# Tokens and memory loaded already turned, beside the plain copies

## The chip, the cores and the metric

The program runs on one NeuronCore of a Trainium2 chip. The metric is the device time of one launch in microseconds (us); its median of 3 runs before the change is 2022.22 us (2019.41 to 2022.70).

## The reference, cut to what matters

256 tokens of 1024 numbers go through a transformer block (`first_block`) and two further layers whose last part picks 16 rows per head and token out of a table of experts. What the change touches is the beginning of the first block:

```
h     = rmsnorm(x, mix_norm_g)          # (256, 1024), g a gain per feature
proj  = h @ w_in                        # queries, keys, values of two attentions, memory queries, gates
mem_n = rmsnorm(mem, mem_norm_g)        # (256, 1024)
mkv   = mem_n @ w_mem_kv                # keys and values of the memory
```

`rmsnorm(x, g)` is x times the inverse root of the mean of its squares, times g. A product needs its left operand with features along the partitions, that is, turned. The kernel multiplies by g (one number a partition in the turned form) before the product and by the inverse root (one number a token) when a product is evicted.

## The kernel before, in words

Tokens are handled as two tiles of 128. A stage is a generator in a program for each engine: `block(0)` and `block(1)` ("B0", "B1") are the first block on one tile each, "G0" (`first_gates`) the gate products of tile 0, "M00" to "M11" the mixers of the later layers. A generator yields between steps. A planner (`make_plan`) runs all generators once on paper with prices for instructions (`Meter`: a transpose 0.16 us at L164, a VectorE operation 0.2 us and 0.00107 us a column, L171) and writes for TensorE, VectorE and ScalarE one fixed order of steps; the same run chooses for each of the 512 expert rows of a partition, which are gathered by GpSimd, when it is fetched, into which buffer (`gather`, L660), and whether TensorE or VectorE adds it up (`on_which`, L589). An engine waits for what a step needs, in that order.

All weights come as slabs of 128 x 2048 numbers (1 MB) through a ring of six, issued by SP in the order in which TensorE takes them; slab n waits until slab n - 6 is used. Small loads are written by hand into SP's program among them, and all of SP's loads land in the order of their issue.

Stage B0 on TensorE (L876): eight dummy products (`turns`, L788, with START[0]) on a blank tile; eight transposes of `x3[:, 0]` through PSUM (`turn_tile`, L796), which VectorE multiplies by the gain and writes to `hT` (L1589); nine more dummies; five column tiles of w_in (two slabs each, `token_tile`); sixteen transposes of memory (L902), which VectorE writes to `memT`; the memory products (L912); normalised heads turned, attention; eight transposes of the second half of x (`early_turns`, L1014, evicted into `x1T`, which shares its place with part of `memT`); then the attention output o is turned and goes through the branch products (L960). `early_products` (L1028) later use `x1T` to begin stage B1's first two column tiles in gaps.

ScalarE squares x for the inverse root (`rms_tile`), and every eviction of a column tile needs it. VectorE makes the rotary angles, sums squares of the heads and norms them; group 2 of these waits for the memory products. SP's first loads (L2361 to L2365) are the identity, x, the gains and other vectors (`vecs`), positions and constants; after the fourth slab come the head gains, masks and memory, after the sixth the second half of x (L2308 to L2313).

Of the kernel before, what the change touches and what calls it, by code (L numbers as in the profile page):

```python
# [14 lines left out]
P = 128  # L15
# [12 lines left out]

EARLY_BANKS = (5, 1)
START, NORM, MIX = (8, 9), (0, 2), (0, 0, 3, 2, 4)  # L30
ADD = ((0, 2), (6, 7), (0, 1), (6, 7))
# [30 lines left out]
class Signals:  # L62
# [24 lines left out]
    def at(self, name, *key):  # L87
        if self.by_name:
            return self.name(name, *key)
        return self.sem(name), self.values.get((name, key), 1)  # L90
# [138 lines left out]
def program(nc, T, out):  # L229
    ctx = ExitStack()  # L230
    with ctx:
# [489 lines left out]
        def tensor_program(pe, measured=False):  # L721
# [154 lines left out]
            def block(t):  # L876
# [9 lines left out]
                if t == 0:  # L886
                    w.wait_ge(sig.sem("blank"), 1)
                    turns(b_[5], START[0], diag[:, 0:128])
                    w.wait_ge(sig.sem("l_id"), 16)
                    yield from turn_tile(s, x3[:, t, :], b_[6:8], "turned_v", (sig.sem("l_x0"), 16), "h")  # L890
                    turns(b_[5], START[1])
                    w.wait_ge(*at("turned_v", s, "h", 1))
                else:
                    w.wait_ge(*at("x1T_over"))
                    w.wait_ge(*at("qkv", 1, 1))
# [4 lines left out]
                if t == 0:  # L900
                    for u in range(2):
                        yield from turn_tile(s, mem3[:, u, :], b_[6:8], "turned_v", (sig.sem("l_m"), 16), "m%d" % u)  # L902
                    w.wait_ge(*at("turned_v", s, "m1", 1))
                    for part in range(2):
                        weights, n = take(s)
                        wk = blocks_of(weights, 4, 512)
                        for u in range(2):
                            b = b_[2 + u]
                            if part == 0:
                                wait_bank(b)  # L910
                            for k in range(4):
                                ins = pe.matmul(bank(b), memT[:, 4 * part + k, 128 * u:128 * u + 128], wk[:, k, :],  # L912
                                                start=(part == 0 and k == 0), stop=(part == 1 and k == 3))
                            if part == 0 and u == 1:
                                ins.then_inc(*up("half", "mem_kv"))
                                consumed[n] = ("half", "mem_kv")
                            if part == 1:
                                ins.then_inc(*up("mem_kv", u))
                                bank_free[b] = at("mem_out", u, 1)
                            yield  # L920
                    consumed[n] = ("mem_kv", 1)

                def heads():
                    w.wait_ge(*at("normed", t))
                    for i, (blocks, _) in enumerate(query_key_groups(s, t)):
                        b = b_[i % 2]
                        wait_bank(b)
                        for j, c in enumerate(blocks):
                            ins = pe.transpose(bank(b)[:, 128 * j:128 * j + 128], raw[:, 128 * c:128 * c + 128], ident)
                        ins.then_inc(*up("qk_turn", t, i))  # L930
                        bank_free[b] = at("qk_out", t, i)
                        yield
                    if t == 0:
                        b = b_[0]
                        wait_bank(b)
                        for i, (j, u) in enumerate(((0, 0), (0, 1), (1, 0), (1, 1))):
                            ins = pe.transpose(bank(b)[:, 128 * i:128 * i + 128], mem_k[:, u, 128 * j:128 * j + 128], ident)
                        ins.then_inc(*up("qk_turn", t, 4))
                        bank_free[b] = at("qk_out", t, 4)
                    yield from attention(s, block_units(s, t), [at("qk_out", t, 4 if t == 0 else 3)])  # L940

                yield from heads()
                if t == 0:
                    early_turns()
                yield from turn_tile(s, scr_[:, 0:1024], b_[6:8], "turned_a", at("att_out", s, 2), "o")
# [67 lines left out]

            def early_turns():  # L1014

                w.wait_ge(sig.sem("l_x1"), 16)
                w.wait_ge(*at("gates_out", 0, 4))
                for h in range(2):
                    b = EARLY_BANKS[h]
                    wait_bank(b)  # L1020
                    for i in range(4):
                        ins = pe.transpose(bank(b)[:, 128 * i:128 * i + 128], x3[:, 1, 512 * h + 128 * i:512 * h + 128 * i + 128], ident)
                    ins.then_inc(*up("turn", "B1", "h", h))
                    bank_free[b] = at("turned_v", "B1", "h", h)

            early_weights = {}

            def early_products(s, c, first, last):  # L1028

                b = room["B1"].bank[c]  # L1030
                for k in range(first, last):
# [4 lines left out]
                    if k == 0:  # L1036
                        w.wait_ge(*at("turned_v", "B1", "h", 1))
                        wait_bank(b)
# [10 lines left out]
            def first_gates():  # L1049

                b_, hTt = room["B0"].bank, hT_tile("B0")
                w.wait_ge(*at("turned_v", "B0", "h", 1))
                for c in range(6):
                    after = at("gates_out", 0, c - 2) if c > 1 else at("mem_out", 1, 1) if c else at("turned_v", "B0", "h", 1)
                    yield from token_tile("G0", (b_[5], b_[3])[c % 2], hTt, "gates", 0, c, after=after)
# [159 lines left out]
        def scalar_program(act, measured=False):  # L1215
# [78 lines left out]
            def block(t):  # L1294
# [6 lines left out]
                else:  # L1301
# [3 lines left out]
                    yield  # L1305
                    yield from rms_tile(s, row_y[0], "h", (sig.sem("l_x1"), 16), at("turned_v", "B0", "m1", 1))
                    begin(s)
# [104 lines left out]
            def mixer(l, t):  # L1412
# [42 lines left out]
                if l == 0:  # L1455
                    before.append(at("turned_v", "B0", "m1", 1))
                else:
                    before.append(at("dot", 128 * t + 127))
# [25 lines left out]
            def recurrence(l, t):  # L1484
# [4 lines left out]
                if l == 0:  # L1489
                    w.wait_ge(*at("turned_v", "B0", "m1", 1))  # L1490
                else:
                    w.wait_ge(*at("dot", 128 * t + 127))
# [66 lines left out]
        def vector_program(v, measured=False):  # L1559
# [29 lines left out]
            def turn_tile(s, key, gain, banks, dst):  # L1589

                for h in range(2):
# [5 lines left out]
                    yield  # L1597
                yield

            def attention(s, t, units, out):  # L1600
# [113 lines left out]
            def block(t):  # L1714
# [5 lines left out]
                if t == 0:  # L1720
                    begin(s)
                    yield from turn_tile(s, "h", vecs[:, V_MIX:V_MIX + 8], b_[6:8], hTt)
                yield from rms_tile(s, "h", "rms", s)
# [80 lines left out]
                if t == 0:  # L1804
                    for u in range(2):
                        yield from turn_tile(s, "m%d" % u, vecs[:, V_MEM:V_MEM + 8], b_[6:8], memT[:, :, 128 * u:128 * u + 128])

# [17 lines left out]
                if t == 0:  # L1825
                    yield from turn_tile("B1", "h", vecs[:, V_MIX:V_MIX + 8], EARLY_BANKS, x1T)
                for br in range(3):
# [438 lines left out]
        def load_program(sp):  # L2266
# [32 lines left out]
            def block(t):  # L2299
# [5 lines left out]
                for c in range(4 if t else 0, 10):  # L2305
                    slab(S_QKV + c)
                    if t == 0 and c == 3:
                        sp.dma_start(rows, T["rows"][:, 0:384]).then_inc(sig.sem("l_r"), 16)  # L2308
                        sp.dma_start(const[:, K_MC:K_ONE], T["const"][:, K_MC:K_ONE]).then_inc(sig.sem("l_k"), 16)
                        sp.dma_start(early[:, 0:1024], T["const"][:, K_END - 1024:K_END]).then_inc(sig.sem("l_k"), 16)  # L2310
                        sp.dma_start(mem3, T["mem"].rearrange("(t p) d -> p t d", p=P)).then_inc(sig.sem("l_m"), 16)
                    if t == 0 and c == 5:
                        sp.dma_start(x3[:, 1, :], x_in[:, 1, :]).then_inc(sig.sem("l_x1"), 16)  # L2313
                    yield
                if t == 0:
# [3 lines left out]
                    for br in range(3):  # L2319
                        yield from branch(br)  # L2320
                    small(0)
                else:
# [37 lines left out]

            sp.dma_start(const[:, 0:K_MC], T["const"][:, 0:K_MC]).then_inc(sig.sem("l_id"), 16)  # L2361
            sp.dma_start(x3[:, 0, :], x_in[:, 0, :]).then_inc(sig.sem("l_x0"), 16)
            sp.dma_start(vecs[:, :], T["vecs"]).then_inc(sig.sem("l_v"), 16)
            sp.dma_start(posi[:, :], T["pos"]).then_inc(sig.sem("l_p"), 16)
            sp.dma_start(const[:, K_ONE:], T["const"][:, K_ONE:K_END - 1024]).then_inc(sig.sem("l_c"), 16)  # L2365
            stage = {"B0": block(0), "G0": first_gates(), "B1": block(1)}
# [168 lines left out]
```

## Time and profile before

| what | value |
|---|---|
| median of 3 runs | 2022.22 us |
| the profiled execution's own time | 2018.75 us |
| its span, first to last instruction | 2016.9 us |
| TensorE matmul busy | 1770.3 us (88%) |
| VectorE busy | 1282.6 us (64%) |
| ScalarE busy | 870.7 us (43%) |
| bytes moved by DMA | 770.14 MB, mean 382 GB/s |

One execution was recorded. Busy times of engines overlap, and a share of the whole span is a mean over stages with different limits; the views by stretch tell which limit holds where. A product of 128 x 512 shows as two matmul records of the trace, a transpose as one.

### The profile page before, as it was taken

How to read it: one execution, taken by the hardware profiler on the slowest of the kernel's cores; microseconds unless marked ns; L12 is line 12 of the kernel's file. 1: busy time of each engine (PE TensorE's matmuls, PEld its weight loads, DVE VectorE, ACT ScalarE, POOL GpSimd, SP SyncE). 2: the span in 40 equal slices, each digit the busy share in tenths (PEclk: the TensorE clock that was granted, in tenths of full speed). 3: DMA queues.
4: the chain of work that ended last, by engine and by line, in shares of the span. 5: the costliest groups of instructions: out<-in, count | busy, mean ns of one | idle time of the engine just before them, and what ended most of it. 6: DMA issues, size and time to landing. Idle time of an engine off the chain costs nothing.

```text
span 2016.9 us, 21790 instructions
## 1 busy us (share of the span) xinstructions
PE 1770.3 (88%) x7152; PEld 1000.8 (50%) x7152; DVE 1282.6 (64%) x3502; ACT 870.7 (43%) x2188; POOL 584.8 (29%) x517
## 2 busy tenths in 40 slices
PE   9999999999899989888779979977898888777776
PEld 5459865764487446455225535622364474222222
DVE  4324337678565448786786857688677688865444
ACT  2423214344488433723344473344445625443333
POOL 0000000033232225334343324344433335443331
PEclk9999999999999989999899999999999989999999
DMA  9669877479999999999999999999999999999996
GB/s 391 217 256 362 299 278 250 161 286 419 419 419 419 420 420 418 419 418 395 419 420 420 419 419 409 419 419 420 420 420 419 379 419 420 420 419 420 420 420 267
DMA packets 108385, 770.14 MB, mean 382 GB/s; under 512 B 12144, under 2 KB 12656, under 8 KB 16368
## 3 DMA queue, kind: packets, MB, share of 16 engines
q0 software_dynamic: 73728, 536.90, 64.4%
q1 hardware_dynamic: 34544, 231.85, 29.7%
q8 instruction: 56, 0.92, 0.2%
q14 instruction: 57, 0.47, 0.1%
HBM read 767.65 MB, written 1.05 MB: 381 GB/s over the span
## 4 chain that ended last, share of the span: by engine, by line
DMA 48%; PE 38%; DVE 6%; ACT 4%; issue 2%; POOL 1%; SPq 0%; DVEq 0%; POOLq 0%; ACTq 0%
DMA arena<-in_peer_dram,eidx 17%; DMA ring<-in_peer_dram,eidx 13%; PE psum L1189 10%; PE psum L754 9%; DMA kv<-in_peer_dram,eidx 9%; PE psum L777 7%; DMA ring<-in_slabs_dram 5%; PE psum L989 5%; DMA early<-in_peer_dram,eidx 4%; PE psum L1006 2%; PE psum L960 1%; DVE ring L2108 1%; DVE arena L2108 1%; ACT diag L1534 1%; PE psum L852 1%
## 5 line engine op out<-in xcount | busy, mean ns | idle before, releaser
L2261 POOL DMA_INDIRECT arena<-in_peer_dram,eidx x205 | 238.0, 1161 | 789.7 <-DVE eidx L1980 409.9
L1189 PE MATMUL psum<-arena,diag 128*128 128x512 f32 x704 | 344.5, 615 | 69.2 <-ACT diag L1534 68.0
L1524 ACT ACTIVATE wexp<-wexp 128x1 f32<-128x1 f32 x512 | 103.2, 201 | 669.6 <-DVE wexp L2108 658.8
L2108 DVE CUSTOM_DVE_ANT_0 arena<-arena,osb 128x1024 f32<-128x1024 f32 x205 | 250.2, 1223 | 147.1 <-DMA arena<-in_peer_dram,eidx 143.7
L1189 PE MATMUL psum<-ring,diag 128*128 128x512 f32 x568 | 277.8, 614 | 55.3 <-ACT diag L1534 54.6
L2261 POOL DMA_INDIRECT ring<-in_peer_dram,eidx x152 | 170.5, 1122 | 281.5 <-PE psum L1189 241.6
L754 PE MATMUL psum<-ring,hT 128*128 128x512 f32 x528 | 241.2, 604 | 11.8 <-DMA ring<-in_slabs_dram 10.4
L1189 PEld LDWEIGHTS psum<-arena,diag 128*128 128x128 f32 x704 | 124.8, 192 | 252.0 <-ACT diag L1534 147.7
L2108 DVE CUSTOM_DVE_ANT_0 ring<-ring,osb 128x1024 f32<-128x1024 f32 x152 | 185.6, 1222 | 100.5 <-DMA ring<-in_peer_dram,eidx 98.8
L1189 PE MATMUL psum<-kv,diag 128*128 128x512 f32 x368 | 184.3, 626 | 41.7 <-ACT diag L1534 37.8
L1189 PEld LDWEIGHTS psum<-ring,diag 128*128 128x128 f32 x568 | 100.9, 192 | 204.0 <-ACT diag L1534 117.6
L1534 ACT ACTIVATE diag<-const,wexp 128x128 f32<-128x128 f32 x455 | 182.6, 401 | 16.3 <-PE psum L1189 1.5
L2261 POOL DMA_INDIRECT kv<-in_peer_dram,eidx x104 | 117.6, 1131 | 241.3 <-PE psum L1189 185.8
L2108 DVE CUSTOM_DVE_ANT_0 kv<-kv,osb 128x1024 f32<-128x1024 f32 x104 | 127.1, 1223 | 86.2 <-DMA kv<-in_peer_dram,eidx 85.5
L777 PEld LDWEIGHTS psum<-hT,ring 128*128 128x128 f32 x1344 | 159.5, 195 | 28.1 <-issue 17.1
L989 PEld LDWEIGHTS psum<-hT,ring 128*128 128x128 f32 x1408 | 162.6, 192 | 14.2 <-issue 8.6
L777 PE MATMUL psum<-hT,ring 128*128 128x128 f32 x1344 | 161.5, 278 | 8.2 <-DMA ring<-in_slabs_dram 6.6
L989 PE MATMUL psum<-hT,ring 128*128 128x130 f32 x1408 | 163.5, 276 | 3.7 <-DMA ring<-in_slabs_dram 1.9
L754 PEld LDWEIGHTS psum<-ring,hT 128*128 128x128 f32 x528 | 98.7, 192 | 133.8 <-issue 111.7
L1527 ACT ACTIVATE wexp<-wexp,sm 128x1 f32<-128x1 f32 x512 | 150.7, 294 | 16.6
L1189 PEld LDWEIGHTS psum<-kv,diag 128*128 128x128 f32 x368 | 66.1, 194 | 141.3 <-ACT diag L1534 80.8
L1524 ACT ACT_TABLE_LOAD x82 | 105.2, 1283 | 1.5
(340 smaller groups left out, 2023.6 us busy)
## 6 DMA issues: line engine op xcount, KB each, us to landing
ring<-in_slabs_dram SPq DMA_DIRECT2D x200, 1024.0 KB, 5.4
ring<-in_slabs_dram SPq DMA_DIRECT2D x8, 768.0 KB, 4.2
kept<-in_slabs_dram SPq DMA_DIRECT2D x4, 1024.0 KB, 13.7
arena<-in_peer_dram,eidx POOLq DMA_INDIRECT x205
ring<-in_peer_dram,eidx POOLq DMA_INDIRECT x152
ring<-in_slabs_dram SPq DMA_DIRECT2D x4, 512.0 KB
kk<-in_keys_dram SPq DMA_DIRECT2D x2, 1024.0 KB
kv<-in_peer_dram,eidx POOLq DMA_INDIRECT x104
```

The lines of the kernel that those rows point to most:

```text
L754: ins = pe.matmul(bank(b), hT_[:, k, :], wk[:, k % 4, :], start=(k == 0), stop=(k == 7))
L777: ins = pe.matmul(bank(b)[:, 128 * i:128 * i + 128], wk[:, k, 128 * (i % 2):128 * (i % 2) + 128], hT_[:, k, :], start=(k == 0), stop=(k == 7))
L852: ins = pe.matmul(bank(b)[:, c0:c0 + 64], p3[:, h, c, :], u.v(h, c), start=(c == 0), stop=(c == nb - 1))
L960: ins = pe.matmul(bank(b), oT[:, k0 + k, :], wk[:, k, :], start=(k == 0), stop=(k == kb - 1))
L989: ins = pe.matmul(bank(b)[:, 256 * gv:256 * gv + 130], wk[:, k, 128 * gv:128 * gv + 128], hTe[:, k, :], start=(k == 0), stop=(k == 7))
L1006: ins = pe.matmul(bank(b), act[:, f, :], wk[:, k, 512 * h:512 * h + 512], start=(f == 0), stop=(f == 21))
L1189: ins = pe.matmul(bank(b), diags_of(n), pair(slot_of[n])[:, 1024 + 512 * h:1536 + 512 * h], start=(k == 0), stop=(k == 127))
L1524: act.activation(wn, wn, ACT.Gelu_apprx_tanh).then_inc(*up("gelu", n))
L1527: act.activation(wn, wn, ACT.Copy, scale=gate[t][:, k:k + 1]).then_inc(*up("weight", n))
L1534: act.activation(diags_of(n), ident, ACT.Copy, scale=wn).then_inc(*up("diag", n))
L2108: v.tensor_tensor_reduce(out=row, in0=row, in1=row_y[t], scale=1.0, scalar=0.0, op0=ALU.mult, op1=ALU.add, accum_out=wexp[:, c:c + 1]).the ...
L2261: pool.indirect_dma_start(pair(i), None, tables, bass.IndirectOffsetOnAxis(ap=eidx[:, 128 * t + k:128 * t + k + 1], axis=0)).then_inc(sig. ...
```

## The change

Two arrays are added to the inputs: x and memory with features along the partitions. TensorE no longer turns inputs; `hT`, `memT` and `x1T` are loaded and then multiplied in place by the gain in one VectorE operation each (`scale_input`). The plain x and memory are still loaded, since the squares and the residual need them. The dummy products become fifteen in one run. Waits on the old evictions become waits on `scaled_in`, or on `mem_sq` where they guard the buffer of plain memory. Small loads change places, and the wait for the identity moves to the heads.

```
+START, NORM, MIX = 15, (0, 2), (0, 0, 3, 2, 4)

 tensor, block(0):
-                    turns(b_[5], START[0], diag[:, 0:128])
-                    w.wait_ge(sig.sem("l_id"), 16)
-                    yield from turn_tile(s, x3[:, t, :], b_[6:8], "turned_v", (sig.sem("l_x0"), 16), "h")
-                    turns(b_[5], START[1])
-                    w.wait_ge(*at("turned_v", s, "h", 1))
+                    turns(b_[5], START, diag[:, 0:128])
+                    w.wait_ge(*at("scaled_in", "x0"))
...
-                    for u in range(2):
-                        yield from turn_tile(s, mem3[:, u, :], b_[6:8], "turned_v", (sig.sem("l_m"), 16), "m%d" % u)
-                    w.wait_ge(*at("turned_v", s, "m1", 1))
+                    w.wait_ge(*at("scaled_in", "mem"))
...
-                if t == 0:
-                    early_turns()

 vector:
+            def scale_input(name, turned, gain, n):
+                w.wait_ge(sig.sem("l_v"), 16)
+                w.wait_ge(sig.sem("l_t" + name), 16)
+                g_ = gain.unsqueeze(2).to_broadcast([P, 8, n])
+                v.tensor_tensor(turned, turned, g_, ALU.mult).then_inc(*up("scaled_in", name))
...
-                    for u in range(2):
-                        yield from turn_tile(s, "m%d" % u, vecs[:, V_MEM:V_MEM + 8], b_[6:8], memT[:, :, 128 * u:128 * u + 128])
+                    scale_input("mem", memT, vecs[:, V_MEM:V_MEM + 8], 256)
+                    yield

 loads, first:
-            sp.dma_start(const[:, 0:K_MC], T["const"][:, 0:K_MC]).then_inc(sig.sem("l_id"), 16)
-            sp.dma_start(x3[:, 0, :], x_in[:, 0, :]).then_inc(sig.sem("l_x0"), 16)
+            sp.dma_start(hT[:, 0:1024], T["xT"][0]).then_inc(sig.sem("l_tx0"), 16)
             sp.dma_start(vecs[:, :], T["vecs"]).then_inc(sig.sem("l_v"), 16)
-            sp.dma_start(posi[:, :], T["pos"]).then_inc(sig.sem("l_p"), 16)
-            sp.dma_start(const[:, K_ONE:], T["const"][:, K_ONE:K_END - 1024]).then_inc(sig.sem("l_c"), 16)

 loads, behind slab c of w_in (0 to 9):
+   c == 1: x (first half), positions, constants
    c == 3: head gains            + identity, memory (masks gone from here)
+   c == 7: memT
-   c == 5: x (second half)
+   c == 9: masks, x (second half)

 loads, behind the last branch slab:
+                    w.wait_ge(*at("mem_kv", 1))
+                    sp.dma_start(arena[:, 7168:8192], T["xT"][1]).then_inc(sig.sem("l_tx1"), 16)
                     small(0)
```

`small(0)` is six loads for the later layers (L2278). Stage B1's scaling of `x1T` stands in VectorE's program where the evictions of `early_turns` stood.

## Rows read from the trace of the kernel before

**Rows 1.** The page: DMA rate in 40 slices; the chain by engine

```profile
GB/s 391 217 256 362 299 278 250 161 286 419 419 419 419 420 420 418 419 418 395 419 420 420 419 419 409 419 419 420 420 420 419 379 419 420 420 419 420 420 420 267
...
DMA 48%; PE 38%; DVE 6%; ACT 4%; issue 2%; POOL 1%; SPq 0%; DVEq 0%; POOLq 0%; ACTq 0%
```

**Rows 2.** Two stretches: length, busy time (instructions) by engine, clock, DMA share, rate

```profile
40.00:60.00 20.00, 20.00 (x60) 9.76 (x59) 10.54 (x25) 0.94 (x3) 0.00 (x0) 1.00 0.82 326
...
100.00:120.00 20.00, 19.21 (x91) 11.74 (x90) 5.17 (x19) 10.86 (x23) 0.00 (x0) 1.00 0.57 191
```

**Rows 3.** Timeline of the start: start, length, engine, line, operation, tiles, idle before

```profile
0.75 0.38 SPq L2361 DMA_DIRECT2D const<-in_const_dram  x1
...
1.00 3.78 PE L794 MATMUL psum<-diag 128*128 128x128 f32 x16 [1.00 <-POOL diag L2247]
1.19 0.42 SPq L2362 DMA_DIRECT2D x<-in_x_dram  x1
...
4.80 1.06 ACT L1223 ACTIVATE scr<-x 128x1024 f32<-128x1024 f32 x1 [2.78 <-DMA x<-in_x_dram]
...
6.65 2.28 PE L794 MATMUL psum<-const 128*128 128x128 f32 x18
...
9.12 13.97 PE L754 MATMUL psum<-ring,hT 128*128 128x512 f32 x32 [0.19 <-DMA ring<-in_slabs_dram]
...
13.31 0.26 ACT L1292 ACTIVATE junk<-junk 128x64 f32<-128x64 f32 x1 [1.54 <-DVE junk L1704]
...
24.11 16.15 PE L754 MATMUL psum<-ring,hT 128*128 128x512 f32 x37 [1.02 <-DMA ring<-in_slabs_dram]
```

**Rows 4.** DMA issues at 0.75, 1.65, 4.0 and 16.2: size, us to landing

```profile
const<-in_const_dram SPq DMA_DIRECT2D x1, 64.0 KB, 1.9
...
vecs<-in_vecs_dram SPq DMA_DIRECT2D x1, 193.0 KB, 3.7
...
ring<-in_slabs_dram SPq DMA_DIRECT2D x1, 1024.0 KB, 10.0
...
ring<-in_slabs_dram SPq DMA_DIRECT2D x1, 1024.0 KB, 17.3
```

**Rows 5.** Chain of waits, 44 to 135 us: start, length, engine and line

```profile
44.98 0.87 PE psum L805 x8
...
115.86 0.88 PE psum L1022 x8
116.73 0.87 PE psum L805 x8
...
132.36 1.72 PE psum L1039 x4
```

**Rows 6.** Timelines of VectorE and SP near 116 us; the issue at 116.3

```profile
115.96 0.42 DVE L1646 TENSOR_TENSOR scr<-psum,sm 128x256 f32<-128x256 f32 x1 [4.74 <-PE psum L852]
...
113.89 0.43 SPq L2282 DMA_DIRECT2D wf<-in_wf_dram  x1
...
115.81 0.98 SPq L2295 DMA_DIRECT2D kept<-in_slabs_dram  x2
...
kept<-in_slabs_dram SPq DMA_DIRECT2D x1, 1024.0 KB, 12.9
```

**Rows 7.** VectorE's groups by shape, 20 to 80 us: busy, mean ns

```profile
L1768 DVE TENSOR_TENSOR scr<-scr,early 128x384 f32<-128x384 f32 x4 | 2.2, 558 | 0.1
...
L1768 DVE TENSOR_TENSOR arena<-arena,early 128x256 f32<-128x256 f32 x2 | 0.9, 426 | 0.1
```

**Rows 8.** Later stretches, columns as in rows 2

```profile
430.00:440.00 10.00, 9.51 (x23) 4.03 (x22) 7.38 (x29) 5.95 (x12) 7.20 (x6) 1.00 1.01 419
...
900.00:930.00 30.00, 28.35 (x196) 23.62 (x197) 20.30 (x67) 6.86 (x21) 8.12 (x7) 1.00 0.95 377
...
1580.00:1610.00 30.00, 26.68 (x78) 12.88 (x78) 21.60 (x33) 15.10 (x39) 9.40 (x9) 0.94 0.93 351
...
2000.00:2017.00 17.00, 7.93 (x16) 2.71 (x16) 7.44 (x16) 5.71 (x15) 0.00 (x0) 0.91 0.10 38
```

More of the change, by code:

```diff
@@ L27 @@
 LAG = 3
-EARLY_BANKS = (5, 1)
-START, NORM, MIX = (8, 9), (0, 2), (0, 0, 3, 2, 4)
+START, NORM, MIX = 15, (0, 2), (0, 0, 3, 2, 4)
 ADD = ((0, 2), (6, 7), (0, 1), (6, 7))
@@ L924, in heads @@
                     w.wait_ge(*at("normed", t))
+                    w.wait_ge(sig.sem("l_id"), 16)
                     for i, (blocks, _) in enumerate(query_key_groups(s, t)):
@@ L1012, in block @@
                     bank_free[b_[6 + h]] = at("ffn_x", t, h)
[L1014 to L1024, printed above, removed]
             early_weights = {}
@@ L1036, in early_products @@
                     if k == 0:
-                        w.wait_ge(*at("turned_v", "B1", "h", 1))
+                        w.wait_ge(*at("scaled_in", "x1"))
                         wait_bank(b)
@@ L1051, in first_gates @@
                 b_, hTt = room["B0"].bank, hT_tile("B0")
-                w.wait_ge(*at("turned_v", "B0", "h", 1))
+                w.wait_ge(*at("scaled_in", "x0"))
                 for c in range(6):
-                    after = at("gates_out", 0, c - 2) if c > 1 else at("mem_out", 1, 1) if c else at("turned_v", "B0", "h", 1)
+                    after = at("gates_out", 0, c - 2) if c > 1 else at("mem_out", 1, 1) if c else at("scaled_in", "x0")
                     yield from token_tile("G0", (b_[5], b_[3])[c % 2], hTt, "gates", 0, c, after=after)
@@ L1305, in block @@
                     yield
-                    yield from rms_tile(s, row_y[0], "h", (sig.sem("l_x1"), 16), at("turned_v", "B0", "m1", 1))
+                    yield from rms_tile(s, row_y[0], "h", (sig.sem("l_x1"), 16), at("mem_sq", 1))
                     begin(s)
@@ L1455, in mixer @@
                 if l == 0:
-                    before.append(at("turned_v", "B0", "m1", 1))
+                    before.append(at("mem_sq", 1))
                 else:
@@ L1489, in recurrence @@
                 if l == 0:
-                    w.wait_ge(*at("turned_v", "B0", "m1", 1))
+                    w.wait_ge(*at("mem_sq", 1))
                 else:
@@ L1721, in block @@
                     begin(s)
-                    yield from turn_tile(s, "h", vecs[:, V_MIX:V_MIX + 8], b_[6:8], hTt)
+                    scale_input("x0", hTt, vecs[:, V_MIX:V_MIX + 8], 128)
+                    yield
                 yield from rms_tile(s, "h", "rms", s)
@@ L1804, in block @@
                 if t == 0:
-                    for u in range(2):
-                        yield from turn_tile(s, "m%d" % u, vecs[:, V_MEM:V_MEM + 8], b_[6:8], memT[:, :, 128 * u:128 * u + 128])
+                    scale_input("mem", memT, vecs[:, V_MEM:V_MEM + 8], 256)
+                    yield
                 yield from norms(1)
@@ L1825, in block @@
                 if t == 0:
-                    yield from turn_tile("B1", "h", vecs[:, V_MIX:V_MIX + 8], EARLY_BANKS, x1T)
+                    scale_input("x1", x1T, vecs[:, V_MIX:V_MIX + 8], 128)
+                    yield
                 for br in range(3):
@@ L2306, in block @@
                     slab(S_QKV + c)
+                    if t == 0 and c == 1:
+                        sp.dma_start(x3[:, 0, :], x_in[:, 0, :]).then_inc(sig.sem("l_x0"), 16)
+                        sp.dma_start(posi[:, :], T["pos"]).then_inc(sig.sem("l_p"), 16)
+                        sp.dma_start(const[:, K_ONE:], T["const"][:, K_ONE:K_END - 1024]).then_inc(sig.sem("l_c"), 16)
                     if t == 0 and c == 3:
                         sp.dma_start(rows, T["rows"][:, 0:384]).then_inc(sig.sem("l_r"), 16)
+                        sp.dma_start(const[:, 0:K_MC], T["const"][:, 0:K_MC]).then_inc(sig.sem("l_id"), 16)
+                        sp.dma_start(mem3, T["mem"].rearrange("(t p) d -> p t d", p=P)).then_inc(sig.sem("l_m"), 16)
+                    if t == 0 and c == 7:
+                        sp.dma_start(arena[:, 6144:8192], T["memT"]).then_inc(sig.sem("l_tmem"), 16)
+                    if t == 0 and c == 9:
                         sp.dma_start(const[:, K_MC:K_ONE], T["const"][:, K_MC:K_ONE]).then_inc(sig.sem("l_k"), 16)
                         sp.dma_start(early[:, 0:1024], T["const"][:, K_END - 1024:K_END]).then_inc(sig.sem("l_k"), 16)
-                        sp.dma_start(mem3, T["mem"].rearrange("(t p) d -> p t d", p=P)).then_inc(sig.sem("l_m"), 16)
-                    if t == 0 and c == 5:
                         sp.dma_start(x3[:, 1, :], x_in[:, 1, :]).then_inc(sig.sem("l_x1"), 16)
@@ L2518 @@
     arrays = {
-        "x": a["x"][0], "mem": a["mem"][0], "pos": a["positions"][0].reshape(2, P).T,
+        "x": a["x"][0], "xT": a["x"][0].reshape(2, P, 8, P).transpose(0, 3, 2, 1).reshape(2, P, 1024),
+        "mem": a["mem"][0], "memT": a["mem"][0].reshape(256, 8, P).transpose(2, 1, 0).reshape(P, 2048), "pos": a["positions"][0].reshape(2, P).T,
         "const": constants(), "vecs": vecs, "rows": np.broadcast_to(row, (P, row.size)),
```

## The prediction

> **What bounds the kernel now.** I read the page's slices first [rows 1]. DMA is below full until about a quarter of the span and then flat at 420 GB/s to the last slice; DMA has 48% of the chain that ended last and TensorE 38%. So there are two regimes, and the change lies wholly in the first. The table by stage [rows 2] shows what the first regime waits for: from 40 to 60 us TensorE is busy for all of 20.00 us and DMA for 0.82, from 100 to 120 us 19.21 us against 0.57. The chain of waits [rows 5] is then one TensorE group behind another, each starting where the last ended, and the only pause before 117 us that a load ends is the 1.02 us ahead of 24.11 us, until a slab of weights had landed [rows 3]. The late windows [rows 8] show the second regime: from 430 us DMA is at 1.01, with a dip at 900 to 930 us (377 GB/s), one at 1580 to 1610 us (351), a small one between, and 17 us at the end with hardly a transfer. There the end is the moment of saturation, plus a fixed number of bytes over the rate, plus dips, plus the tail. A microsecond won ahead of 430 us is won at the end, provided the dips stay as they are.
>
> **The start.** Time now goes, by [rows 3, 4], into a first come, first served queue: the first load, 64 KB, is issued at 0.75 us and takes 1.9; x of 512 KB is issued at 1.19 and ScalarE starts on it at 4.80; vecs is there at 1.65 + 3.7 = 5.35. The third slab, issued at 4.0, takes 10.0 us and is there at 14.0. A megabyte costs 2.5 us at 420 GB/s (estimate from [rows 1]), so slab 0 is there at about 9.0, and TensorE's products begin at 9.12 after an idle 0.19 us. Afterwards turned x takes the first place, one issue slot (0.44 us) earlier than x had: 4.35 us, with 4.0 and 4.8 as ends (without the 64 KB, 0.15 us, and a little of the slow first microseconds; as late as x now). vecs follows at 4.85, slab 0 2.55 us later at 7.4 (7.0 to 8.0). VectorE scales turned x in one 128x1024 product. Nothing in this stretch has that shape; two products of the same kind out of SBUF [rows 7] give a slope, (558 - 426)/128 = 1.03 ns a column, with 0.16 us ahead, so 1.22 us (and 2.27 us for 128x2048). It ends at 6.1, before slab 0. The fifteen dummy products are 30 records (16 records stand for 8 now); at the first rate, 16 in 3.78 us [rows 3], they end at about 7.4, and less if the rate doubles midway as it does now (18 records in 2.28 us). So the eight transposes go for free, and products begin at 7.5 instead of 9.12: 1.6 us.
>
> How much is kept is up to the queue. The slabs and loads ahead of slab 4 are, after slab 0: slab 1 (9.9), x (11.15), pos and constants (0.95, from vecs' 5.35 to the constants' 6.3 now), slab 2 (14.6), slab 3 (17.1), rows (0.47), identity (0.15), mem (2.5), slab 4 at 22.75. A slab feeds 3.49 us of products (13.97 us for four, [rows 3]), so TensorE is through four slabs at 21.6 with a touch of waiting on slab 2, and waits for slab 4 until 22.8. Now it is 24.11. **Term: -1.3 us**, ends -0.7 and -2.0.
>
> x as it is lands 6.35 us later than now. On ScalarE the squares, the root and two sines stand ahead of the first eviction: now 4.80 to 13.57, 8.8 us [rows 3]; from 11.15 that is 20.0, and the eviction (0.69 us) ends at 20.7. TensorE wants that bank for its third column tile at 22.8. It costs nothing with 2 us to spare; were the spare gone, each microsecond would be one on TensorE.
>
> **The turns of memory.** Two groups of eight transposes, at 44.98 (shown) and 47.57 us, cost 0.87 us of the chain each [rows 5], with nothing beside it on TensorE, so they are worth 1.74 us where TensorE bounds. VectorE's four evictions (2.6 us) become one product of 2.27 us that waits for turned memory alone; it lands at about 32.8, VectorE comes to it after the sums over column 3, near 41, and is through before 43.7, when TensorE arrives (22.8 + 20.87). Behind it on VectorE is only the next norm, whose products TensorE asks for much later. The price is in the queue: turned memory (2.5 us) and, newly here, the masks and second half of x (3.1 us) are ahead of slab 10. Without lost time slab 10 is there at 43.4, in time. The queue now lost 0.9 us after slab 5: slab 7, issued at 16.2 and 17.3 us under way [rows 4], is there at 33.5, and 27.8 + 5.0 would be 32.8, with 0.2 more later. Repeated, TensorE waits 0.6. I take the middle, +0.3. **Term: -1.74 + 0.3 = -1.45 us**, ends -1.1 and -1.74. Ahead of 118 us this makes about -2.75.
>
> The gate products that filled the gaps between those turns will be done later, under attention; TensorE's sum is the same.
>
> **The turn of the second half of x.** 0.88 us go at 115.86 [rows 5]. But it stands where TensorE would wait anyway: the turn of o, next in order, needs VectorE's last attention output, which runs 115.96 to 116.38 [rows 6], and starts at 116.73. Only 0.2 us at most can be won; I take **-0.1**.
>
> Its load is not free. SP now issues turned x (0.5 MB) behind the sixth branch slab at 113.5 and ahead of six loads (113.89 to 116.79, [rows 6]). Its new wait, for the memory products, is over since 64 us, so nothing behind it is held up. All later ones land 1.25 us later. The last of them, issued at 116.3, takes 12.9 us and is there at 129.2, and the slab behind it, which TensorE wants at 132.36 (1.72 us on L1039, [rows 5]), at 131.7. The slack is 0.5 to 0.66 us; 1.25 more plus the 0.1 just won turns it into a wait of about 0.75. **Term: +0.75 us**, ends 0.6 and 0.85. The scaling of that half (1.22 us instead of two evictions of 0.69) is done before the first branch product comes out.
>
> **Sum.** -1.3 - 1.45 - 0.1 + 0.75 = -2.1; some 0.2 us I leave to pauses between groups that stay. **-1.9 us** at 136 us and, with the order of later work as it is, at 430 and at the end. Against the profiled execution's own 2018.75 us (span 2016.9, 1.85 around it) that is 2016.85. The median shown is 2022.22, 3.5 above it, so I forecast 2020.3.
>
> **A rule weighed.** By [rows 2] weight loads fill only 9.76 of 20.00 us while matmuls fill all. The Trainium skill, "Perfetto Trace Analysis", section "Identifying the Most-Contended Engine", says that matmul busy time is not a good measure of TensorE's nearness to its limit, and to judge by the weight loads' busy share. Read so, TensorE has half its time free at 45 us, and the turns hide in it: rival three below. Against it stands the chain's order: 0.87 us pass between two groups of products at each turn.
>
> **Rivals.** *One, the planner decides anew and ends worse (slower).* Engines follow an order that a planner makes from prices: 0.16 us for a transpose (L164), so 32 of them, 5.12 us, go from TensorE's account, and VectorE's falls by 1.0; choices for all 512 rows (L589, L660) compare such clocks. Place: the second regime. Price: the dips. By [rows 8] they miss 30 x 43/420 = 3.1 us and 30 x 69/420 = 4.9 us, with the small one (some 1.5) about 9.5. Doubled, the end is -1.9 + 9.5: 2026.4 on the profile's scale, 2029.8 on the median's. It is slower once the dips grow by more than 1.9 us, and measurably so from 5.9. For it: dips are where rows are late for reasons of order. Against: all work after 136 us has the same durations and a nearly even shift. *Two, the new order closes dips*: all closed, -11.4, or 2010.8; half, 2015.6. *Three, TensorE has room:* if weight loads, at half its time in [rows 2], were what fills it, the turns would lie beside products already and their going would win nothing: -1.9 + 1.45, 2021.8. *Four, the late load hides:* no wait at 132 us, and the ends of the start and memory terms: -2.0 - 1.74 - 0.2 = -3.9, 2018.3.
>
> **How the numbers follow.** The forecast has 0.42 (its own range, 2018.5 to 2021.5), rival one 0.22, two 0.24, three 0.07, four 0.05. A measurement tells 0.2%, 4 us, from no change: 2018.2 to 2026.3 is the same. Faster gets nearly all of two (0.22), half of four and a little of the forecast, 0.28; slower 0.20 of one and 0.02 of three, 0.22; the same 0.50. The range goes to rival one's doubled dips and to nearly all of rival two: 2011.5 to 2029.
>
> **What would show it.** Products beginning near 7.5 us and a pause before slab 4 that ends near 22.8; no L805 between 40 and 60 us, memory products from 44 us; a turn of o only 2.8 us earlier than now; a wait for a slab ahead of L1039 near 130. DMA at its plateau 2 us earlier with the dips at the same places would confirm the rest. I am wrong if the first evictions hold TensorE up at 22 us, if a gap opens where memory's scaling waits, or if the dips move: then the early terms may hold and the end not follow them.

## The result and the profile after

The changed kernel takes 2026.41 us (median of 10 runs, 2025.12 to 2031.50) beside 2021.26 for the kernel before (10 runs): ratio 1.003, 95% interval 1.0022 to 1.0038. It is slower by 0.3%, where I had forecast no measurable change with a small gain. The profiled execution after took 2027.52 us with a span of 2025.7, which is 8.8 us above the span of before.

The early gain is there. Timeline of TensorE after (start, length, engine, line, operation, tiles, idle before), for [rows 3, 5]:

```profile
1.00 5.51 PE L793 MATMUL psum<-diag 128*128 128x128 f32 x30 [1.00 <-POOL diag L2237]
9.26 13.97 PE L753 MATMUL psum<-ring,hT 128*128 128x512 f32 x32 [2.75 <-DMA ring<-in_slabs_dram]
24.11 2.41 PE L753 MATMUL psum<-ring,hT 128*128 128x512 f32 x5 [0.88 <-DMA ring<-in_slabs_dram]
...
48.33 13.90 PE L906 MATMUL psum<-ring,arena 128*128 128x512 f32 x32
...
114.78 1.09 PE L804 MATMUL psum<-const,scr 128*128 128x128 f32 x8 [0.59 <-DVE scr L1634]
...
130.46 1.88 PE L1020 MATMUL psum<-ring,arena 128*128 128x512 f32 x4
```

The products begin at 9.26 us, the slab that ended the pause lands at 24.11 as before, the memory products start at 48.33, the turn of o starts at 114.78 (before 116.73 in the chain), and L1020 (L1039 before) at 130.46 instead of 132.20, with no wait. So TensorE is 1.74 us ahead, and GpSimd's first gather of expert rows, at 409.10 instead of 410.84 us, still is. What follows is not. Timeline of GpSimd around the 129th gather (row 128, the first of the second tile), first before, then after; the length is the issue's:

```profile
890.31 0.94 POOL L2261 DMA_INDIRECT kv<-in_peer_dram,eidx  x1 [0.30 <-issue]
916.90 1.28 POOL L2261 DMA_INDIRECT kv<-in_peer_dram,eidx  x1 [25.66 <-DVE eidx L1980]
```

```profile
891.85 0.94 POOL L2251 DMA_INDIRECT arena<-in_peer_dram,eidx  x1 [0.30 <-issue]
930.69 1.28 POOL L2251 DMA_INDIRECT kv<-in_peer_dram,eidx  x1 [37.90 <-DVE eidx L1970]
```

The first tile's last row is fetched 1.5 us later than before, and the second tile's first row 13.8 us later: it waits for `eidx`, the row numbers that VectorE writes when that tile is routed (M01). Meanwhile there are too few transfers to fill the DMA engines. Stretches of before and then after, columns as in [rows 2]; the last figures of a row are the DMA share and the rate in GB/s:

```profile
0.00:430.00 430.00, 418.89 (x2227) 288.08 (x2228) 192.71 (x688) 135.96 (x298) 6.17 (x11) 0.99 0.74 270
430.00:1980.00 1550.00, 1327.65 (x4878) 704.63 (x4876) 1072.63 (x2784) 721.79 (x1852) 575.80 (x503) 0.98 1.01 417
850.00:945.00 95.00, 80.85 (x405) 54.34 (x405) 74.06 (x186) 30.29 (x88) 37.53 (x30) 0.96 0.99 405
```

```profile
0.00:430.00 430.00, 415.96 (x2195) 284.23 (x2196) 193.77 (x686) 136.21 (x300) 7.66 (x12) 0.99 0.76 277
430.00:1980.00 1550.00, 1330.07 (x4878) 707.79 (x4876) 1062.29 (x2769) 719.86 (x1845) 559.34 (x500) 0.97 1.00 414
850.00:945.00 95.00, 72.44 (x393) 51.18 (x392) 70.27 (x177) 29.74 (x78) 29.43 (x26) 0.90 0.88 355
...
900.00:930.00 30.00, 26.73 (x210) 23.89 (x208) 23.21 (x83) 5.92 (x16) 0.00 (x0) 1.00 0.67 268
...
1580.00:1610.00 30.00, 28.46 (x105) 15.29 (x104) 17.78 (x36) 22.53 (x52) 6.58 (x7) 0.97 0.99 385
```

The same for 1550 to 1650 us, before and then after:

```profile
1550.00:1650.00 100.00, 84.25 (x382) 53.41 (x383) 75.49 (x180) 51.15 (x124) 33.75 (x30) 0.93 0.99 399
```

```profile
1550.00:1650.00 100.00, 82.21 (x328) 46.50 (x327) 68.56 (x137) 56.86 (x132) 35.81 (x30) 0.93 0.97 390
```

Up to 430 us DMA moves 7 x 430 us = 3.0 MB more; 2.1 MB of that are the new turned arrays, so 0.9 MB, about 2 us, is the gain. From 430 to 1980 us it loses 3 GB/s x 1550 us / 420 = 11 us. The rates are whole numbers, so this figure can be off by up to 4 us; within that, 11 - 2 agrees with the 8.8 of the spans. Most of the loss is one place: 850 to 945 us at 355 instead of 405 GB/s is 50 x 95 / 420 = 11.3 us. The dip of [rows 8] at 900 to 930 us went from 377 to 268 GB/s. That at 1580 to 1610 us is shallower but longer: from 1550 to 1650 us together another 2 us go, 390 instead of 399 GB/s. The page's slices, for [rows 1], show the large loss in the 17th to 19th, 405, 401 and 330 where before had 419, 418 and 395:

```profile
GB/s 393 250 269 363 300 279 230 174 303 418 419 420 419 420 420 419 405 401 330 420 420 419 419 419 420 419 420 419 420 419 419 366 414 419 421 419 420 420 420 283
```

Why routing is late stands in two timelines. Routing begins when TensorE has made scores of the tile against the keys (L1155 before, L1136 after); VectorE picks the best of them (MAX8) and works out `eidx`. TensorE's scores, in groups of which the first is shown with the fourth, before and then after:

```profile
895.95 1.06 PE L1155 MATMUL psum<-kk,tmp 128*128 128x128 f32 x8
...
931.98 1.05 PE L1155 MATMUL psum<-kk,tmp 128*128 128x128 f32 x8
```

```profile
899.11 1.06 PE L1136 MATMUL psum<-kk,tmp 128*128 128x128 f32 x8
...
927.23 1.05 PE L1136 MATMUL psum<-kk,tmp 128*128 128x128 f32 x8
```

VectorE from the first scores to `eidx`, before and then after:

```profile
897.05 0.50 DVE L1903 MAX8 sm<-psum 128x8 f32<-128x128 f32 x2 [1.55 <-PE psum L1155]
...
915.94 0.19 DVE L1980 TENSOR_TENSOR eidx<-junk 128x32 uint32<-128x32 f32 x1
```

```profile
900.20 0.50 DVE L1893 MAX8 sm<-psum 128x8 f32<-128x128 f32 x2 [0.35 <-PE psum L1136]
...
918.72 1.28 DVE L2108 SCALAR_TENSOR_TENSOR x<-kv,wexp,x 128x1024 f32<-128x1024 f32 x1 [2.16 <-ACT wexp L1508]
920.12 1.28 DVE L2108 SCALAR_TENSOR_TENSOR x<-arena,wexp,x 128x1024 f32<-128x1024 f32 x1
...
928.32 1.28 DVE L2108 SCALAR_TENSOR_TENSOR x<-arena,wexp,x 128x1024 f32<-128x1024 f32 x1 [3.73 <-PE psum L1136]
...
929.73 0.19 DVE L1970 TENSOR_TENSOR eidx<-junk 128x32 uint32<-128x32 f32 x1
```

VectorE starts on the first scores only 3.15 us later than before (900.20 instead of 897.05). The other 10.6 us lie on VectorE itself: from there to `eidx` it takes 29.5 us instead of 18.9. Each fetched expert row costs a dot product and, unless TensorE adds it up, an addition to x on VectorE. Before, four dot products of the first tile's rows stand between the steps of routing. After, there are five, and three additions of such rows to x besides (L2108), and ahead of two of these additions VectorE sits idle for 2.16 and 3.73 us. The profile puts the second wait down to TensorE's fourth group of scores; these came earlier than before (927.23 instead of 931.98), but before nothing ahead of `eidx` waited for them.

Stage B1, ahead of M01, ends late too, but that is not where the time goes. Its last products (L999; L1006 before) end in a group that starts at 745.7 us after and 727.3 before, and of these 18.4 us all but some 3 are made up by the first scores (operation; duration min, median, max in ns, first and last start in us).

```profile
L999 PEld LDWEIGHTS psum<-ring,scr x176: 186/190/190, 233.0 to 745.7; 128*128 128x128 f32 x176
```

```profile
L1006 PEld LDWEIGHTS psum<-ring,scr x176: 186/190/190, 234.7 to 727.3; 128*128 128x128 f32 x176
```

### The profile page after: what moved, and what is told of

It is laid out like the page before. It is cut to its first block, busy times and chain, and to the rows that moved or that the text cites. A ratio compares the mean times of both kernels' runs of the same rounds, so it can differ in the third digit from the quotient of the medians.

```text
span 2025.7 us, 21751 instructions
## 1 busy us (share of the span) xinstructions
PE 1775.9 (88%) x7132; PEld 1002.2 (49%) x7132; DVE 1277.1 (63%) x3493; ACT 872.1 (43%) x2192; POOL 572.7 (28%) x517
## 4 chain that ended last, share of the span: by engine, by line
DMA 49%; PE 33%; DVE 6%; issue 6%; ACT 4%; POOL 2%; SPq 0%; DVEq 0%; POOLq 0%; ACTq 0%
DMA ring<-in_peer_dram,eidx 18%; DMA arena<-in_peer_dram,eidx 13%; DMA kv<-in_peer_dram,eidx 12%; PE psum L1170 8%; PE psum L776 7%; PE psum L753 6%; PE psum L982 4%; DMA ring<-in_slabs_dram 3%; PE psum L999 2%; DMA early<-in_peer_dram,eidx 2%; DVE arena L2098 1%; DVE ring L2098 1%; DVE kv L2098 1%; PE psum L851 1%; ACT diag L1515 1%
## 5 line engine op out<-in xcount | busy, mean ns | idle before, releaser
L2251 POOL DMA_INDIRECT arena<-in_peer_dram,eidx x205 | 227.5, 1110 | 799.8 <-DVE eidx L1970 408.1
L1170 PE MATMUL psum<-arena,diag 128*128 128x512 f32 x704 | 349.5, 621 | 69.5 <-ACT diag L1515 69.0
L982 PEld LDWEIGHTS psum<-hT,ring 128*128 128x128 f32 x1408 | 162.6, 191 | 13.8 <-issue 12.8
L1170 PE MATMUL psum<-early,diag 128*128 128x512 f32 x188 | 94.5, 626 | 25.5 <-ACT diag L1515 25.3
```

The source lines that it names most:

```text
L982: ins = pe.matmul(bank(b)[:, 256 * gv:256 * gv + 130], wk[:, k, 128 * gv:128 * gv + 128], hTe[:, k, :], start=(k == 0), stop=(k == 7))
L1170: ins = pe.matmul(bank(b), diags_of(n), pair(slot_of[n])[:, 1024 + 512 * h:1536 + 512 * h], start=(k == 0), stop=(k == 127))
L2251: pool.indirect_dma_start(pair(i), None, tables, bass.IndirectOffsetOnAxis(ap=eidx[:, 128 * t + k:128 * t + k + 1], axis=0)).then_inc(sig. ...
```

## Experiments

Theory: the time was lost by the order that the planner wrote for the later work, not by the loads or the turns. Rivals: the loads themselves cost it; or the dips have another cause than the moment of routing. The first four kernels ran on one chip, with the kernel before at 2020.73 us (21 runs).

**The old kernel with the new order, and the reverse.** A price that exists on the planner's paper alone, with no instruction behind it, is enough to make it write the other kernel's order: in the traces all 512 gathers go into the same buffers in the same sequence as in the other kernel.

```
 before_new_order (before):          after_old_order (after):
+  if measured and t == 0:          +  if measured and t == 0:
+      pe.run(1.0)                  +      pe.run(0.2)
```

> The kernel before, with 1.0 us added on paper to TensorE's price of stage B0 and no instruction or load changed. The planner then writes the same order of expert rows (gathers, buffers, TensorE or VectorE) as for the changed kernel. Theory order: the loss is that order alone, so this is slower than before by the loss and by the early gain that the changed kernel has and this one lacks: 2021.3 + 5.2 + 1.7 = about 2028 us; row 128 is gathered about 14 us after where the kernel before has it and DMA misses about 22 us at the plateau where now it misses 10. Rival, the loads and VectorE products themselves cost it: 2021.3 us, dips as before.

> The changed kernel, with 0.2 us added on paper to TensorE's price of stage B0 and nothing else. The planner then writes the order of expert rows that the kernel before has. Theory order: the early gain of 1.74 us reaches the end, 2019.5 us, dips as before and 1.7 us earlier. Rival, the loads cost it: 2026.4 us as the changed kernel.

Measured: before_new_order 2031.77 us, ratio 1.005 (1.0037 to 1.0064); after_old_order 2018.87, ratio 0.9989 (0.9980 to 0.9998). So the order costs 11.0 us with the old loads (2031.77 - 2020.73) and 7.5 with the new (2026.41 - 2018.87, from two sets of runs); the loads win 1.9 at the old order (2020.73 - 2018.87) and 5.4 at the new (2031.77 - 2026.41, two sets again). before_new_order is 3.8 us above the 2028 that I expected; in its profile the first gather is at 414.10 us, 3.3 later than before, which I have not traced. The gathers of row 128 go with the order, whichever the loads (before_new_order first):

```profile
936.35 1.28 POOL L2263 DMA_INDIRECT kv<-in_peer_dram,eidx  x1 [39.17 <-DVE eidx L1982]
```

```profile
917.01 0.94 POOL L2253 DMA_INDIRECT kv<-in_peer_dram,eidx  x1 [24.45 <-DVE eidx L1972]
```

The theory holds, and the rival that the loads cost the time falls.

**Other prices.** The kernel before with two other paper prices of a transpose:

```
 L164, before_price_158:              before_price_150:
-        return self.run(0.16)       -        return self.run(0.16)
+        return self.run(0.158)      +        return self.run(0.15)
```

> The kernel before with a transpose priced at 0.158 us instead of 0.16 on paper; a third order of the rows, and no instruction changed. Theory order: another draw from the orders, somewhere in 2018 to 2032 us, as likely slower as not, with the difference in DMA's dips. Rival, orders are worth no more than a microsecond: 2021.3 us.

> The kernel before with a transpose priced at 0.15 us on paper; a fourth order of the rows. Theory order: 2018 to 2032 us, the difference in DMA's dips. Rival, orders are worth no more than a microsecond: 2021.3 us.

Measured: 2028.36 us (ratio 1.0037, 1.0024 to 1.0051) and 2021.80 (1.0002, 0.9993 to 1.0011). In their profiles row 128 is gathered at 925.86 and 919.62 us, and 850 to 945 us run at 373 and 414 GB/s. A price 2 ns lower costs 7.6 us, one 10 ns lower nothing clear of noise: the time does not follow the price in one direction. Orders jump; no edit that moves the paper's clock can be taken to leave the order alone.

**The pace at which the planner calls rows late.** B1 and M01 are put ahead of sums of rows as soon as the rows still to be summed, times T_PACE, are less than the work left in these stages. The changed kernel with two other paces (kernel before in that set: 2020.72, 21 runs):

```
 L35, after_pace_33:      after_pace_40:
-  T_PACE = 3.5           -  T_PACE = 3.5
+  T_PACE = 3.3           +  T_PACE = 4.0
```

> The changed kernel with its own loads, and one figure of the planner changed: the pace at which rows are called late, 3.3 us a row instead of 3.5. What it tests: that it is the planner's order that lost the time, through the moment at which the second tile of the first routing (M01) is done, and not something in the new order's details. Theory: late rows are called later, steps of stage B1 and of M01 come before the sums of rows, row 128 is gathered at about 912 to 918 us instead of 930.7, the dip of DMA at 900 to 930 us goes back to some 3 us or less, and the time is 2015 to 2020 us (I say 2018). Rival: the dips do not follow from the moment of routing: row 128 may be early, but the lost transfer time stays at some 22 us and the time at 2025 to 2028.

> The same with 4.0 us a row, the other way. Theory: sums of rows are put first more often, M01 routes at 930 us or later (930 to 942), the lost transfer time of DMA is 22 to 28 us and the kernel takes 2026 to 2033 us (I say 2029). Rival: the moment of routing does not follow the pace or does not set the time: anything else, 2018 to 2024 with row 128 later than 925 above all.

Measured: 2019.39 us (0.9992, 0.9983 to 1.0001) and 2031.66 (1.0050, 1.0035 to 1.0066). At 3.3 the row numbers of the second tile are there at 902.84 us, before the first tile's rows are all fetched, and GpSimd waits for buffers instead of routing; at 4.0 they are the releaser again. VectorE's and GpSimd's timelines at 3.3, GpSimd's at 4.0:

```profile
902.84 0.19 DVE L1970 TENSOR_TENSOR eidx<-junk 128x32 uint32<-128x32 f32 x1
...
915.25 0.94 POOL L2251 DMA_INDIRECT ring<-in_peer_dram,eidx  x1 [4.28 <-PE psum L1170]
```

```profile
930.79 1.26 POOL L2251 DMA_INDIRECT arena<-in_peer_dram,eidx  x1 [35.23 <-DVE eidx L1970]
```

The stretch 850 to 945 us at 3.3 and at 4.0:

```profile
850.00:945.00 95.00, 80.14 (x391) 54.13 (x389) 68.91 (x197) 29.32 (x82) 33.58 (x29) 0.93 1.00 412
```

```profile
850.00:945.00 95.00, 78.66 (x424) 56.70 (x423) 72.84 (x189) 37.47 (x93) 30.14 (x25) 0.91 0.85 342
```

With early routing the dip is gone (412 GB/s) and 7 us are back; with late routing it is deeper. Eight kernels side by side, from one profile each, with the median of their runs:

| kernel | VectorE starts on the first scores | from there to `eidx` | row 128 | 850 to 945 us | median |
|---|---|---|---|---|---|
| before | 897.05 us | 18.9 us | 916.90 us | 405 GB/s | 2020.73 us |
| after_old_order | 897.05 | 19.0 | 917.01 | 414 | 2018.87 |
| before_price_150 | 899.76 | 18.9 | 919.62 | 414 | 2021.80 |
| after_pace_33 | 883.94 | 18.9 | 915.25 | 412 | 2019.39 |
| before_price_158 | 899.70 | 25.2 | 925.86 | 373 | 2028.36 |
| after | 900.20 | 29.5 | 930.69 | 355 | 2026.41 |
| after_pace_40 | 908.44 | 21.4 | 930.79 | 342 | 2031.66 |
| before_new_order | 904.16 | 31.2 | 936.35 | 353 | 2031.77 |

The four slow kernels are those with a late row 128 and a deep dip, and in each of them additions of first-tile rows stand between the steps of routing, in the other four none. That speaks against the rival that the dips have another cause. The moment of routing alone is not isolated, since every order differs in other places too: after and after_pace_40 gather row 128 at the same moment and are 5 us apart.

**Why the first slab was late.** Two kernels on top of after_old_order, one run each:

```
 hold_behind_slab0, behind slab 0:              hold_until_slab0:
+  w.wait_ge(sig.sem("l_tx0"), 16)             +  w.wait_ge(sig.sem("slab%d" % place(0)), 16)
```

> after_old_order, but SP waits until turned x is there before it issues anything behind slab 0. What it tests: why slab 0 came at 9.13 us and not at the 7.4 that I had worked out. Theory: DMA engines that are done with their part of slab 0 go on with later loads, and the slowest engine's part is held up by the traffic: with nothing behind it slab 0 lands at 7.4 to 7.9 us and the products begin there (the load of slab 1 is then about 0.7 us later than in after). Rival: the first loads are slow by themselves, whatever follows them: slab 0 at 8.9 to 9.4 as before. One look, so no verdict on the whole time; about 2018 to 2021.

> after_old_order, but SP issues nothing behind slab 0 until slab 0 itself is there. hold_behind_slab0 still let slab 1 in from 4.4 us, and slab 0 came at about 9.4. What it tests: whether traffic behind slab 0 is what makes it late. Theory (other loads take engine time that slab 0's slowest engine needs): with none at all behind it slab 0 is there at 7.0 to 8.0 us. Rival (the slowest engine's part is late by itself): 8.9 to 9.5 us. In both the whole kernel is slower than after_old_order by what slab 1 comes later: TensorE is through slab 0 3.5 us after it lands, and slab 1 needs some 4.5 us from its issue, so about 1 us and a few more for the slabs behind it: 2020 to 2024.

Products began at 9.46 and 9.18 us (single runs of 2020.2 and 2022.42 us). Even with nothing at all issued behind slab 0, its rate falls off well before it is there (stretches of hold_until_slab0):

```profile
6.00:7.00 1.00, 0.17 (x2) 0.00 (x0) 0.17 (x1) 0.00 (x0) 0.00 (x0) 1.00 0.79 328
7.00:8.00 1.00, 0.00 (x0) 0.00 (x0) 0.00 (x0) 0.00 (x0) 0.00 (x0) 1.00 0.21 90
8.00:9.00 1.00, 0.00 (x0) 0.00 (x0) 0.00 (x0) 0.00 (x0) 0.00 (x0) 1.00 0.08 33
```

The share of 0.21 is about three of 16 engines. The trace's records of the slab's 128 packets, 8 KB each, say the same: they form 16 trains of eight, each packet starting where the one ahead ended. Thirteen trains start between 3.98 and 4.65 us and are through by 7.12; three start only at 5.74 to 5.79, and the last of them ends at 8.70. My theory that later traffic holds the slab up falls: three engines come to it more than a microsecond late, with nothing behind it. Why they do stays open.

**The pause ahead of slab 0, and the masks.** The first kernel is after_old_order with one edit, the second is the first with one more:

```
 after_old_start26:
-START, NORM, MIX = 15, (0, 2), (0, 0, 3, 2, 4)
+START, NORM, MIX = 26, (0, 2), (0, 0, 3, 2, 4)
 masks_late, loads of block(0):
-  behind slab 9 of w_in:              masks (two loads), x (second half)
+  behind the first memory slab:       masks (two loads), x (second half)
```

> The changed kernel with the old order of later work (after_old_order) and 26 dummy products in place of 15. What it tests: whether the pause of TensorE between the dummies and the first slab costs time. In after the dummies ended at 6.5 us and slab 0 was there at 9.1, a pause of 2.75 us without loss in that profile; in after_old_order the same pause (2.87 us) was followed by a granted clock of 0.50 from 10 to 15 us and products at 0.85 us instead of 0.43, about 2.1 us lost. Theory: the pause is what lets the clock fall, in some executions; with dummies up to about 9.0 us the clock is 1.00 from there on in all of them, first products still at 9.1 to 9.6, and the median lies 0 to 2 us (I say 1) below after_old_order's 2018.9: 2018. Rival: the fall is not due to the pause, or is rare: 2018.9 as before, and some profiles still show 0.50 near 10 us. Second rival: the dummies run past slab 0 and push the products by up to 0.5 us: 2019.4.

> after_old_start26 (old order of later work, 26 dummy products), with the masks and the second half of x (1.3 MB) issued behind the first slab of the memory weights instead of behind slab 9. What it tests: the price that I gave to their place. In after_old_start26 TensorE waited 1.04 us at 45.46 us for a slab that lands behind these loads. Theory: the wait goes, the memory products start at 48.0 instead of 49.0, nothing else waits for the masks or for x before 70 us, and the profile's first gather comes 1 us earlier (409 instead of 410); the median is about 1 below after_old_start26's 2019.3, 2018.3, which five rounds can hardly tell. Rival: the slab is late for another reason (time lost in the queue), and the wait stays at 0.5 us or more.

In after_old_order the pause of 2.87 us was followed by a clock of 0.50; with 26 dummies there is no pause and the clock stays at 1.00 (10 to 15 us, after_old_order and then after_old_start26; the third figure from the end):

```profile
10.00:15.00 5.00, 5.00 (x7) 1.88 (x7) 0.32 (x2) 1.71 (x3) 0.00 (x0) 0.50 1.03 419
```

```profile
10.00:15.00 5.00, 5.00 (x13) 2.14 (x12) 0.36 (x3) 2.69 (x5) 0.00 (x0) 1.00 1.03 418
```

The median did not follow: 2019.28 us (0.9991, 0.9982 to 1.0000) beside 2018.87. Either the clock falls in few executions, or the wait at 45.46 us takes the gain back; the runs do not tell. That wait is the one that masks_late removes (TensorE, after_old_start26 and then masks_late):

```profile
45.46 3.70 PE L753 MATMUL psum<-ring,hT 128*128 128x512 f32 x8 [1.04 <-DMA ring<-in_slabs_dram]
49.00 1.45 PE L908 MATMUL psum<-ring,arena 128*128 128x512 f32 x3
```

```profile
23.31 24.30 PE L753 MATMUL psum<-ring,hT 128*128 128x512 f32 x56 [0.53 <-DMA ring<-in_slabs_dram]
47.45 2.74 PE L908 MATMUL psum<-ring,arena 128*128 128x512 f32 x6
```

Of the 1.55 us by which the memory products start earlier, 1.04 are the wait; slab 0 also came earlier there (products at 8.88 us instead of 9.43). masks_late takes 2017.45 us beside 2021.19 for the kernel before there (15 runs): ratio 0.9984, interval 0.9975 to 0.9993. It is faster than the kernel before by 0.16%, 3.7 us, and so than the changed one too. after_old_start26 won 1.4 us in its own set of runs; the wait explains about one of the 2.3 us between them, the rest is not separated from the two sets' difference.

## Why the prediction was wrong

The step that failed is "with the order of later work as it is, at 430 and at the end". The order did not stay: with the new loads the new one costs 7.5 us (2026.41 beside 2018.87), with the old loads 11.0. Rival one happened, with the mechanism that it was given: dips that grow because rows are late for reasons of order. That its price comes out nearly right, 9.5 us where some 11 were lost, is luck: I had doubled all dips, while one grew from 3.1 to 10.9 us of missed transfers (900 to 930 us at 268 GB/s) and the others changed by some 2 at most. I gave this rival 0.22 and argued against it that "all work after 136 us has the same durations and a nearly even shift". That is no argument about a planner: it saw 5.12 us less of TensorE's time on paper, and the other orders show that 1.0 or 0.2 us there are enough, in either direction: 1.0 more in the old kernel gives the order that the change gave, 0.2 more in the changed kernel gives the old one back. I also named the place only as "the second regime". The profile could have told more: the gap of 25.66 us ahead of row 128 waits for routing, and it is there that a reordering can lose 11 us at once.

The early terms, one by one:

- **Start, -1.3 us: measured 0.** Turned x landed at 4.41 us (I had 4.35) and its scaling took 1.23 us (1.22), but slab 0 was there at 9.2 instead of 7.4. I charged its megabyte at the plateau's 420 GB/s, as if all 16 engines began on it together; in hold_until_slab0 three of them begin more than a microsecond late. The dummies ended at 6.5 and not 7.4, so the pause was longer than any that I had reckoned with, and slab 4 ended the next one at 24.11 as before.
- **Memory, -1.45: measured -1.67** (50.00 to 48.33). The turns' 1.74 held nearly in full and the wait for slab 10 did not come, but partly because the start had won nothing: TensorE reached that slab at some 45 us, not at 43.7. It did come in after_pace_33, where the start was 0.8 us ahead, with 0.32 us, and in after_old_start26 with 1.04, beyond my upper end of 0.6. The gate products between the turns were not put off as I had said: they still stand ahead of the memory products, which begin at 48.33 and not at 44; the sum does not change by it.
- **Second half of x, -0.1: about that.** TensorE now waits 0.59 us for VectorE's `scr` ahead of the turn of o, the cover that I had named.
- **Its load, +0.75: measured 0.** The lead at L1020 is 1.74 us and no wait stands ahead of it. I had let the load of 0.5 MB push all later ones back by 1.25 us, but from 112 to 116 us the DMA engines were mostly idle, so it went into unused time. SP was also through with the slab ahead 1.66 us earlier than before, and so issued the loads behind turned x 1.2 us earlier (the first at 112.69 instead of 113.89 us). The stretch before and then after:

```profile
112.00:116.00 4.00, 4.00 (x27) 3.07 (x26) 0.04 (x1) 1.98 (x3) 0.00 (x0) 1.00 0.37 79
```

```profile
112.00:116.00 4.00, 3.28 (x27) 2.78 (x25) 0.42 (x1) 1.56 (x4) 0.00 (x0) 1.00 0.73 227
```

- **Sum at 136 us, -1.9: measured -1.74**, right by luck, by errors that cancel: 1.3 too much won at the start, 0.75 too much lost at the load, 0.2 too little won at memory and 0.2 left to pauses.

At the old order the whole change is worth -1.9 us by the medians, which is the forecast's size; the forecast's condition was wrong, and its sum came out right by the same luck. Rival two fell (the dips grew), rival four's late load did hide but without its start term. Rival three fell: by the Trainium skill, "Perfetto Trace Analysis", section "Identifying the Most-Contended Engine", which names the weight loads' busy share beside a figure of arithmetic done, a share of one half would leave TensorE room; here memory's turns, 1.74 us, came out of the chain nearly whole (1.67).

## What to carry to other kernels

Where instructions are ordered by a program from prices, an edit has two effects, its own and that of the order that comes out; separate them by giving both kernels each order before judging the edit. In a stage bound by transfers look first for the gap in which nothing can be issued until a late result is there, and ask of each edit what it does to that result's place in the order. Follow that result back on every engine: here it was late by what stood between its own steps on VectorE, more than by what came ahead of them.

## What the hardware showed

- A load is there when the slowest of 16 DMA engines has done its part, and engines can start on one load far apart: in hold_until_slab0, with nothing behind slab 0, thirteen began on it between 3.98 and 4.65 us and three at 5.74 to 5.79. The thirteen were through by 7.12 us, the three by 8.70, and the products began at 9.18.
- TensorE's granted clock fell to 0.50, the lower of its two levels (1.2 of 2.4 GHz), in some profiles after a pause ahead of slab 0: after pauses of 2.87, 2.62, 2.01 and 1.95 us (after_old_order, hold_behind_slab0, before_price_150, after_pace_40), not after 3.00, 2.75, 1.62, 1.49 and 1.16 (hold_until_slab0, after, after_pace_33, before_price_158, before_new_order). The pause's length alone does not decide it.
